# Feed-forward products of 256 columns in place of 512, in two halves of the tokens

## What is computed

```
h2 = rms_norm(x, norm2_g[l])
x = x + jnp.square(jax.nn.relu(h2 @ w_ff_up[l])) @ w_ff_down[l]
...
def _mlp(x, norm_g, w1, w2):
    h = _rmsnorm(x, norm_g)
    return jnp.square(jax.nn.relu(h @ w1)) @ w2
```

## Time and profile before

| what | value |
|---|---|
| median of 2 runs | 2823.52 us (2823.07 to 2823.96) |
| span of the profiled execution | 2827.7 us |
| TensorE matmuls busy | 2698.2 us, 12908 of them |
| VectorE busy | 1344.5 us |
| ScalarE busy | 1086.4 us |
| moved by DMA | 204.64 MB, 72 GB/s over the span |

### The profile page before, as it was taken

The page is one execution under the profiler, slowest core; times in us unless marked ns, Lnnn a source line. Parts: engine busy times, 40 slices in busy tenths (PEclk is TensorE's granted clock), DMA queues, the critical chain, the costliest instruction groups (busy, mean ns, idle before and its releaser), DMA issues. The chain is left out here.

```text
span 2827.7 us, 34281 instructions
## 1 busy us (share of the span) xinstructions
PE 2698.2 (95%) x12908; PEld 2066.8 (73%) x12908; DVE 1344.5 (48%) x2079; ACT 1086.4 (38%) x1742; POOL 46.7 (2%) x87
## 2 busy tenths in 40 slices
PE   7999999987899999999999899999999999899999
PEld 5777777766687888865656688887676777688887
DVE  4443444566555444446444644444354445644443
ACT  5444445445633222344434422223343334422222
POOL 2000000000000000001010000000000000000000
PEclk8999999998999999999979999999999999999999
DMA  4211112212232333320100233332222221233332
GB/s 120 60 53 53 45 49 77 70 51 55 60 97 82 97 96 96 97 60 23 31 23 23 68 97 96 96 96 82 70 66 66 75 78 46 79 101 95 97 96 71
DMA packets 397022, 204.64 MB, mean 72 GB/s; under 512 B 7171, under 2 KB 395349, under 8 KB 396902
## 3 DMA queue, kind: packets, MB, share of 16 engines
q1 hardware_dynamic: 396300, 202.97, 25.2%
q10 hardware_dynamic: 601, 0.06, 0.0%
HBM read 200.91 MB, written 2.10 MB: 72 GB/s over the span
## 5 line engine op out<-in xcount | busy, mean ns | idle before, releaser
L878 DVE TENSOR_TENSOR wlo<-raw,whi 128x1024 fp32r<-128x1024 f32 (+1 forms) x399 | 468.7, 1175 | 1030.5 <-ACT whi L844 527.3
L1340 PE MATMUL psum<-hhi,whi 128*128 128x512 f32 x1976 | 809.9, 410 | 36.4 <-DVE hlo L1281 26.4
L1340 PE MATMUL psum<-hlo,whi 128*128 128x512 f32 x1976 | 807.3, 409 | 0.0
L1340 PE MATMUL psum<-hhi,wlo 128*128 128x512 f32 x1976 | 789.9, 400 | 0.0
L1340 PEld LDWEIGHTS psum<-hhi,whi 128*128 128x128 f32 x1976 | 378.4, 191 | 138.6 <-issue 42.5
L1340 PEld LDWEIGHTS psum<-hhi,wlo 128*128 128x128 f32 x1976 | 378.4, 192 | 103.0 <-issue 25.8
L1340 PEld LDWEIGHTS psum<-hlo,whi 128*128 128x128 f32 x1976 | 379.9, 192 | 87.1 <-issue 17.5
L1340 PE MATMUL psum<-uhi,whi 128*128 128x512 f32 x1056 | 417.4, 395 | 4.5 <-DVE ulo L1100 3.6
L1340 PE MATMUL psum<-uhi,wlo 128*128 128x512 f32 x1056 | 417.8, 396 | 0.0
L1340 PE MATMUL psum<-ulo,whi 128*128 128x512 f32 x1056 | 417.5, 395 | 0.0
L604 ACT COPY stage<-psum 128x512 f32<-128x512 f32 x214 | 125.1, 585 | 580.7 <-PE psum L1340 577.2
(11 more groups left out here) (194 smaller groups left out, 2049.7 us busy)
## 6 DMA issues: line engine op xcount, KB each, us to landing
raw<-in_w_in_dram SPq DMA_DIRECT2D x77, 512.0 KB, 3.8
raw<-in_w_mlp_in_dram SPq DMA_DIRECT2D x64, 512.0 KB, 4.1
raw<-in_w_mlp_out_dram SPq DMA_DIRECT2D x64, 512.0 KB, 3.7
raw<-in_w_in_o_dram SPq DMA_DIRECT2D x48, 512.0 KB, 3.8
raw<-in_w_ff_up_dram SPq DMA_DIRECT2D x32, 512.0 KB, 4.1
raw<-in_w_ff_down_dram SPq DMA_DIRECT2D x32, 512.0 KB, 3.8
raw<-in_w_in_e_dram SPq DMA_DIRECT2D x18, 512.0 KB, 3.8
raw<-in_w_gla_branch_dram SPq DMA_DIRECT2D x8, 512.0 KB, 3.8
```

The lines of the kernel that those rows point to most:

```text
L878: dve.tensor_tensor(wlo[:, u % 4, 0:kt, :], raw[:, u % 4, 0:kt, :], whi[:, u % 4, 0:kt, :].bitcast(F32), ALU.subtract).then_inc(lo_done, 1)
L1340: mm = pe.matmul(g, w[:, u % 4, k, :], v[:, k, :], start=n == 0, stop=n == 3 * kt - 1)
```

## The change

In the feed-forward stages TensorE takes a unit's 512 tokens in two halves. The first half runs through all 8 pieces of k with 256 columns per product, then the second half does the same, in the other 256 columns of the same PSUM bank. `half_products` takes the place of `products` there. A unit has 48 matmuls of 256 columns instead of 24 of 512. The waits for the normed pieces and for the posted up units stand in the first half only. The unit is told done after the last product of the second half. The other stages and the other engines' programs are as before.

```diff
+            def half_products(u, k, half, hi, lo):
+
+                c = slice(256 * half, 256 * half + 256)
+                g = psum[:, u % 2, c]
+                if u in norm_before and half == 0:
+
+                    pe.wait_ge(norm_lo, KD * norm_before[u] + k + 1)
+                for part, (w, v) in enumerate(((whi, hi), (whi, lo), (wlo, hi))):
+                    mm = pe.matmul(g, w[:, u % 4, k, :], v[:, k, c], start=k == 0 and part == 0,
+                                   stop=k == KD - 1 and part == 2)
+                if k == KD - 1 and half == 1:
+                    mm.then_inc(unit_done, 1)
...
                     for j in range(16):
                         u = b + j
                         begin(u, f * 16)
-                        for k in range(KD):
-                            if j == 8:
-
-                                pe.wait_ge(posted, b + k + 1 + f * 16)
-                            products(u, 3 * k, 3 * k + 3, *((hhi, hlo) if j < 8 else (uhi, ulo)))
+                        for half in range(2):
+                            for k in range(KD):
+                                if j == 8 and half == 0:
+
+                                    pe.wait_ge(posted, b + k + 1 + f * 16)
+                                half_products(u, k, half, *((hhi, hlo) if j < 8 else (uhi, ulo)))
```

## The result

The changed kernel takes 2958.5 us (median of 2 runs, 2954.5 to 2962.5) against 2823.5: ratio 1.0494, 95% interval 1.0453 to 1.0534. Run again beside another set of the kernel before it gave 1.0491 (1.0453 to 1.0530). The forecast was 2930 us, slower, in a range of 2858 to 2970. The profiled execution of the changed kernel has a span of 2952.5 us, 124.8 us above that of before.

A forecast was written before the change was run, and what follows sets the result against it. TensorE, busy 95% of the span mostly with line 1340's products, was taken as the bound; 61 us (products) + 27 (up-down wait) + 7 (after norms) + 11 (clock) = 106 on 2823.5 gave 2930 us, range 2858 to 2970.

The forecast's parts named there:

- The fixed price of a product: Feed-forward products: 13.3 ns paid once per product whatever its width, so a half costs 120 ns; adds 61 us.
- The rivals' 113, 116 and 128 ns: Other prices of a half product: mostly per column (chance 0.20), as f32 (0.15), load and product in step (0.11).
- in-step rival: Load and product without slack, each half some 8 ns more, 128 ns; 177 us in all, 3000 us; chance 0.11.
- The wait between up and down: Unit 8 of each pass reaches k = 7 early and stalls 2.42 us; 2.24 us extra in 12 places, 27 us.
- The first unit after a norm: 27 half products left after the last normed piece in place of 3 products; 2.24 us extra at 3 stages, 7 us.
- The clock: Stretches at 1.2 GHz, 1.6 us each, behind one stall of three and once more per norm; 11 us, bounds 0 and 24.
- The fetch: Feed-forward loop body, grown to 1536 loads and products, fetched again in 9 later passes at 3.5 us; chance 0.08.
- refetch rival: Instructions fetched again in each of 9 later passes, 31 us on top of the forecast, 2962 us; chance 0.08.

The follow-up runs named there:

- e5: Changed kernel with units 0 and 8 of each pass in whole 512-column products, the other 14 in halves; 2875.1 us, ratio 1.0202.
- e4: Kernel before, with up units 1 to 6 of each pass cut into products of other widths, 64 to 448 columns; 2933.8 us in a single run.
- e3: Changed kernel, but at position 8 of a pass VectorE posts unit 7 before making the low weights of unit 10; 2911.4 us, ratio 1.0314.
- e6: Kernel before (512 columns), with unit 8 waiting for unit 7 after 12 products in place of 21; 2854.2 us, ratio 1.0146.
- e1: Changed kernel with 12 tiny f32 products (48 instructions) at TensorE's start, moving where the loop bodies lie; 2927.1 us, ratio 1.0382.
- e2: Changed kernel with 90 instructions added at TensorE's start (22 tiny products and a transpose); 2966.8 us in a single run.

## Why the prediction was right

**The fixed price of a product: right.** "I take the fixed price of 120 ns": 120.0 measured, and e5 shows 52.7 us for 7/8 of the products, so 61 for all. The rivals' 113, 116 and 128 ns are out. The choice between 113 and 120 could not be settled by a trace in which every product of this format had 512 columns; e4 settles it. That the right value was taken owes something to luck: of the two reasons given, one, that the extra is there whether or not a load runs beside the product, had no row behind it, since every product of every run has a load; the other, that f32 has a fixed part too, points to 116, and f32 was a poor neighbour. The in-step rival's 8 ns do not follow from its row either (0.24 against 0.227 us), which changes nothing in the forecast.

**The wait between up and down: right.** Forecast a stall of 2.42 us, 2.24 more than before, in 12 places; measured 2.42, and 2.20 more per pass. e3 and e6 confirm the chain as its cause from both sides.

**The first unit after a norm: right.** 27 half products stand behind the last hlo. Half of them run at 1.2 GHz, as TensorE's timeline in ff1 of the changed kernel shows, where the earlier trace rows had the full clock:

```profile
1669.66 0.41 PE L1352 MATMUL psum<-hlo,whi 128*128 128x256 f32 x1
...
1672.43 0.37 PE L1352 MATMUL psum<-hhi,wlo 128*128 128x256 f32 x1
1672.64 0.28 PE L1352 MATMUL psum<-hhi,whi 128*128 128x256 f32 x1
```

Fourteen starts in 2.98 us are 213 ns each, and only then come the 120 ns. From the first product after the last hlo to the end of the unit the three stages take 4.64, 5.21 and 5.14 us, where they took 0.80 each: 12.6 us more. The sum had 12.5 for this: 6.7 for the wait, 4.8 for the clock and 1.0 of the 61.

**The clock: mis-sized.** The sum had 11 us: one stall of three, and one stretch per norm. It was two of three (8 of 12), at the norms two to four stretches more, and 6.8 us at 0.50 around each fetch. Its share follows from the stages: 134.5 less 61.4 of products, 26.9 of stalls, 6.7 behind the norms and 19.6 of fetches (20.0 of distances less three products) leaves 20 us. Some 5 of them lie behind the norms, as forecast: there were more stretches than the one forecast, but much of their time fell on waits. The other 15 lie in the passes, where the sum had 6. The price of a stretch was right, 1.48 us measured against 1.6; their number was not. 8 stalls are 12 us, and the remaining 3 or so belong to the fetches, for which the sum had nothing.

**The fetch: a rival that came true in one stage, next to the forecast.** The rival had 9 turns at 3.5 us. It was 3 turns at 6.7 us: a third of the places, and twice the price, since TensorE stood through two transfers in a row. The trace of before fetched nothing in later passes and could not tell, since its bodies are half as long. The Trainium skill (Runtime: NRT & Kernel Launch, section Instruction fetch mechanics) gives TensorE 2048 instructions, by which a body of 1571 stays. The trace agrees for two of three places and disagrees for one. Why 6.14 pieces should not stay in room for eight is not shown. Runs e1 and e2 show that it hangs on where the body lies, and the measurement decides.

So 106 us of forecast against 134.5 in the stages are short by 20 for the fetches and 9 for the clock. The other four fifths of the loss came as worked out. That the time still lies in the stated range owes something to the refetch rival, which had set its upper end.

Taking both halves of each k in turn, so that 42 half products would stand ahead of k = 7, was not tried in unit 8; that it would remove the stall is not shown.

## What to carry to other kernels

A matmul's price here is a slope and a fixed part. In fp32r, each product with its own weight load, the fixed part is 13.3 ns, 6% of a full product and 11% of a half one: use the widest product that fits. An order of loops is also a schedule: whoever halves the work ahead of a wait must ask how long the chain behind the wait is, and a stall costs more than its length: those of 2.1 to 2.8 us here were followed in 2 to 10 of 12 cases by 3.4 us at half clock, some 1.5 us lost each time. A loop body that grows can be fetched again in every pass, in one place of the program and not in another.

## What the runs showed that was not expected

- A body of 1571 instructions was fetched again in each pass when it lay in one place (ff0, or ff2 after 90 instructions more) and not in the others, at 6.2 to 7.4 us of idle TensorE per turn; moving it by 48 instructions took 26 of 112 transfers away and some 1% of the time. A reason that fits all runs is a body that reaches over 8 pieces of 256 instructions in place of 7, and e2 was forecast with it. It is not shown: the records give the distances between the bodies, not where a body begins in a piece.
- The fixed part of an fp32r product does not depend on whether the weights differ from the ones before, as long as they are loaded again, and 448 columns cost 202.5 ns, 2.5 more than the line.
- l2, whose code no run edited, took between 370 and 387 us in these profiles, by how much of it fell at 1.2 GHz. On this kernel a difference of under 10 us in one span says little, and stages have to be compared.
